# A three-layer transformer forward pass: one attention head, the gates, the turns and the first roundings are given other places in a hand-written order

## What is computed

```python
for layer in range(2):                       # layers one and two
    u = rms_norm(x, attn_norm_w) @ w_in
    o_main = silu(g) * rms_norm(retention(q, k, v))        # layer one, 6 heads
    o_main = rms_norm(diff_attention(q, k, v, lam))        # layer two, 6 heads: softmax(map 0) - lam * softmax(map 1)
    o_mem = memory_attention(qc, mk, mv)                   # both, 4 heads
    x = x + concat([o_main, o_mem]) @ w_out
    x = x + (silu(gate) * up) @ w_down                     # gate, up from rms_norm(x) @ w_gate_up
# layer three
z, xbc, dt, q, k, v, f = split(rms_norm(x) @ w_in_2)
y_ssd = ssd_mixer(silu(causal_depthwise_conv(xbc)), z, dt) # 4 taps, 16 heads
y_fox = fox_mixer(q, k, v, f)                              # 16 heads
x = x + concat([y_ssd, y_fox]) @ w_out_2
x = x + conv_gated_mlp(rms_norm(x))
```

## Time and profile before

| | |
|---|---|
| median of three runs | 1065.42 us |
| the profiled execution | 1065.32 us, its span 1063.5 us |
| TensorE busy | 1042.3 us, 98% of the span |
| VectorE busy | 747.6 us, 70% |
| ScalarE busy | 606.4 us, 57% |
| POOL busy | 155.9 us, 15% |
| data read from HBM | 172.39 MB |

### The profile page before, as it was taken

One profiled execution on the slowest core, in us unless ns is written; L12 is line 12 of the kernel. 1 busy time (PEld: TensorE's weight loads), 2 busy tenths in 40 slices (PEclk: granted clock), 3 DMA queues, 4 the chain that ended last, 5 costly groups with the idle time before them and its releaser, 6 DMA issues.

```text
span 1063.5 us, 23813 instructions
## 1 busy us (share of the span) xinstructions
PE 1042.3 (98%) x8638; PEld 1007.7 (95%) x8638; DVE 747.6 (70%) x1244; ACT 606.4 (57%) x1095; POOL 155.9 (15%) x160
## 2 busy tenths in 40 slices
PE   6999999999999999999999999999999999999998
PEld 6989999999999888999999999999888999999998
DVE  6875886666555877965665549878867479998743
ACT  7654764454544766744445446665766667666532
POOL 2200031111110000311111110000101034454300
PEclk9999999999999999999999999999999999999999
DMA  7533555555655332555555664444233455555563
GB/s 292 179 137 92 168 182 186 185 180 175 190 172 184 133 100 80 181 196 178 186 185 168 190 198 141 165 154 139 95 115 103 147 178 182 191 180 177 175 206 96
DMA packets 51767, 174.43 MB, mean 164 GB/s; under 512 B 5872, under 2 KB 7152, under 8 KB 51568
## 3 DMA queue, kind: packets, MB, share of 16 engines
q1 hardware_dynamic: 51696, 173.46, 49.9%
HBM read 172.39 MB, written 1.05 MB: 163 GB/s over the span
## 4 chain that ended last, share of the span: by engine, by line
PE 52%; DVE 6%; ACT 2%; issue 1%; ACTq 0%; DVEq 0%
PE bank L741 10%; PE bank L742 9%; PE bank L743 9%; PE scores L741 6%; PE scores L742 6%; PE scores L743 6%; DVE ring_lo L1588 2%; DVE xw_lo L1594 1%; ACT tmp L1390 1%; PE scores L947 0%; PE bank L1053 0%; PE bank L970 0%; DVE tmp L1725 0%; DVE x L1686 0%; DVE negmax L1964 0%
## 5 line engine op out<-in xcount | busy, mean ns | idle before, releaser
L1588 DVE TENSOR_TENSOR ring_lo<-ring_raw,ring_hi 128x1024 fp32r<-128x1024 f32 (+2 forms) x340 | 402.7, 1188 | 63.4 <-ACT ring_hi L1120 57.8
L1120 ACT ACTIVATE ring_hi<-ring_raw 128x1024 fp32r<-128x1024 f32 (+2 forms) x340 | 341.3, 1008 | 80.5 <-PE bank L743 39.3
L741 PE MATMUL bank<-xw_hi,ring_hi 128*128 128x256 f32 x1048 | 302.6, 289 | 1.6 <-DVE ring_lo L1588 0.6
L742 PE MATMUL bank<-xw_lo,ring_hi 128*128 128x256 f32 x1048 | 296.3, 283 | 0.0
L743 PE MATMUL bank<-xw_hi,ring_lo 128*128 128x256 f32 x1048 | 296.1, 283 | 0.0
L741 PEld LDWEIGHTS bank<-xw_hi,ring_hi 128*128 128x128 f32 x1048 | 200.5, 191 | 8.1 <-issue 5.1
L742 PEld LDWEIGHTS bank<-xw_lo,ring_hi 128*128 128x128 f32 x1048 | 200.7, 191 | 0.1
L743 PEld LDWEIGHTS bank<-xw_hi,ring_lo 128*128 128x128 f32 x1048 | 200.6, 191 | 0.0
L741 PE MATMUL scores<-xw_hi,ring_hi 128*128 128x256 f32 x528 | 150.1, 284 | 0.1
L742 PE MATMUL scores<-xw_lo,ring_hi 128*128 128x256 f32 x528 | 149.4, 283 | 0.0
L743 PE MATMUL scores<-xw_hi,ring_lo 128*128 128x256 f32 x528 | 149.4, 283 | 0.0
(11 more groups left out here) (238 smaller groups left out, 1792.1 us busy)
## 6 DMA issues: line engine op xcount, KB each, us to landing
ring_raw<-w_up SPq DMA_DIRECT2D x132, 512.0 KB, 3.2
ring_raw<-w_in SPq DMA_DIRECT2D x85, 512.0 KB, 3.3
ring_raw<-w_down SPq DMA_DIRECT2D x48, 512.0 KB, 3.6
ring_raw<-w_down SPq DMA_DIRECT2D x24, 384.0 KB, 3.8
ring_raw<-w_oa SPq DMA_DIRECT2D x24, 256.0 KB, 2.7
ring_raw<-w_ob SPq DMA_DIRECT2D x12, 512.0 KB, 4.1
ring_raw<-w_oa SPq DMA_DIRECT2D x8, 512.0 KB, 3.9
ring_raw<-w_kv SPq DMA_DIRECT2D x7, 512.0 KB, 6.6
```

The source lines that it names most:

```text
L741: mm(bank[b][:, 0:T], w_hi, tile(hi, t), start=kk == 0, stop=False)
L742: mm(bank[b][:, 0:T], w_hi, tile(lo, t), start=False, stop=False)
L1120: A(ring_hi[:, slot * DM:slot * DM + width], ring_raw[:, slot * DM:slot * DM + width], ACT.Copy).then_inc(hi_done, 1)
L1588: V.tensor_tensor(ring_lo[:, a:b], ring_raw[:, a:b], ring_hi[:, a:b].bitcast(f32), SUB).then_inc(lo_done, 1)
```

## The change

- Start: the third tile of `kv` is loaded before the parameters and constants, and ScalarE rounds it after two squares and not after four.
- Layer one: `weights_copy` of the memory heads one slot sooner; `gated` of the second and third pair two slots later (slots 21 and 22 become 23 and 24), their `mix_high` and `mix_low` two and three slots later.
- Layer two: for the sixth head the maxima and the softmax move from before the evacuation or behind the rounding to `MIDDLE`, the copy of the turned weights moves from slot 23 to slot 21 of ScalarE, and the last pair's `mix_low` goes before the rounding of its step.
- `project_group`: in the first `ob` tile both outputs take the first two of their four inputs, then both take the last two.
- Layer three: TensorE turns a tile in the middle of the product tile, not at its end. ScalarE's copies are now called `turn_copy` and stay in their slots.

```diff
-                    at(layer, slot + 2, "weights_copy", "mem", 2 * pair)
+                    at(layer, slot + 1, "weights_copy", "mem", 2 * pair)
...
-        at(0, 20 + half_, "gated", half_)
-        at(0, 21 + half_, "mix_high", 2 * half_)
-        at(0, 21 + half_, "mix_low", 2 * half_)
+        at(0, 22 + half_, "gated", half_)
+        at(0, 23 + half_, "mix_high", 2 * half_)
+        at(0, 24 + half_, "mix_low", 2 * half_)
...
-            plan[1][turned + 1].insert(0, ("weights_copy", "diff", h))
+            at(1, soft, "weights_copy", "diff", h)
...
-        at(2, 4 + t, "turn", 8 + t)
+        at(2, 3 + t, "turn", 8 + t)
+        at(2, 4 + t, "turn_copy", 8 + t)
...
             load_kv(1)
+            load_kv(2)
             sp.dma_start(par[:, streams:NPARAM], params_in[:, streams:NPARAM]).then_inc(par_loaded, 16)
...
-            load_kv(2)
...
-                    for j in range(ph.group):
+                    cuts = (0, ks // 2, ks) if c == 0 else (0, ks)
+                    for k0, k1 in zip(cuts, cuts[1:]):
+                        for j in range(ph.group):
...
-            HALFWAY = (("spread", "turned"), ("spread", "turned"), ("spread", "ssd_out", "small_turn", "fox_turned"))
+            HALFWAY = (("spread", "turned"), ("spread", "turned"), ("spread", "ssd_out", "small_turn", "fox_turned", "turn"))
...
-            for g in range(1, AHEAD):
+            for g, squares_ in ((1, range(0, 2)), (2, range(2, KT))):
...
-            MIDDLE = {"group_out", "norm_mid"}
+            MIDDLE = {"group_out", "norm_mid", "mix_low_mid", "maxima_mid", "softmax_mid"}
```

More of the change, by code:

```diff
@@ L263, in plans @@
         at(1, last, "values", "diff", h)
-        for m in range(2):
-            plan[1][soft].insert(0, ("softmax", "diff", h, 1 - m))
         if h == 5:
+            at(1, soft, "softmax_mid", "diff", h, 0)
+            at(1, soft, "softmax_mid", "diff", h, 1)
             plan[1][turned].insert(0, ("turned", "diff", h))
-            plan[1][turned + 1].insert(0, ("weights_copy", "diff", h))
+            at(1, soft, "weights_copy", "diff", h)
         else:
+            for m in range(2):
+                plan[1][soft].insert(0, ("softmax", "diff", h, 1 - m))
             at(1, turned, "weights", "diff", h)
@@ L539, in program @@
                     k = (layer, *key)
-                    same = {"group_norm": "norm", "weights_copy": "weights", "maxima": "scores"}
+                    same = {"group_norm": "norm", "weights_copy": "weights", "maxima_mid": "scores"}
                     count(same.get(kind, kind), (kind, *k) if kind in ("norm", "group_norm") else k)
@@ L752, in project_group @@
                     pe.wait_ge(lo_done, g + 1)
-                    for j in range(ph.group):
[L754 to L770, removed]
+                    cuts = (0, ks // 2, ks) if c == 0 else (0, ks)
+                    for k0, k1 in zip(cuts, cuts[1:]):
+                        for j in range(ph.group):
+                            m = ph.group * c + j
+                            n = ph.out0 + m
+                            b = bank[ph.bank_of[n]][:, 0:T]
+                            if k0 == 0:
+                                pe.wait_ge(out_ready, ph.freed_out(n))
+                            for k in range(k0, k1):
+                                t = ph.inputs[k]
+                                if m == 0:
+                                    pe.wait_ge(*mixed(layer, t))
+                                a = slot * DM + (j * ks + k) * P
+                                w_hi, w_lo = ring_hi[:, a:a + P], ring_lo[:, a:a + P]
+                                mm(b, w_hi, tile(act_hi, t), start=k == 0, stop=False)
+                                mm(b, w_hi, tile(act_lo, t), start=False, stop=False)
+                                last = mm(b, w_lo, tile(act_hi, t), start=False, stop=k == ks - 1)
+                            if k1 == ks:
+                                last.then_inc(ob_done if j < ph.group - 1 else tile_done, 1)
             def mean_square(q):
@@ L1439, in _ @@
             DO = {"softmax": softmax, "values": values, "fox_probs": fox_probs, "fox_values": fox_values,
-                  "mix_high": mix_high, "weights_copy": weights, "maxima": scores, "small_tok": small_tok, "fox_copy": fox_weights,
-                  "squares": squares, "norm": norm, "group_norm": group_norm, "turn": turn, "decays": decays, "slopes": slopes,
+                  "mix_high": mix_high, "weights_copy": weights, "maxima_mid": scores, "softmax_mid": softmax, "small_tok": small_tok, "fox_copy": fox_weights, "turn_copy": turn,
+                  "squares": squares, "norm": norm, "group_norm": group_norm, "decays": decays, "slopes": slopes,
                   "ret_out": ret_out, "gate_silu": gate_silu, "scores": scores, "weights": weights, "mix": mix,
```

11 lines of the change are left out of this document (6 added, 5 removed).

## The result

The changed kernel takes 1079.24 us (median of four runs, 1076.49 to 1080.18) where the kernel before took 1065.28 us beside it (1064.85 to 1066.02): 14.0 us more, a ratio of 1.0126 with a 95% interval of 1.0106 to 1.0146. Forecast was 1075.2 us, at most 1078.5. The direction and the loop in layer three came as predicted; the time lies 4 us over the forecast and 0.7 us outside its range.

What follows compares the result with a forecast made beforehand. TensorE's products were taken as the bound (busy 1042.3 of 1063.5 us). 1065.3 + 12.7 - 2.4 - 0.5 - 0 - 0 = 1075.1 us profiled, 1075.2 us against the median; 80% range 1072.8 to 1078.5 us.

Steps and rivals of the forecast that it cites:

- The loop: Layer three: each mid-tile turn waits for ScalarE's copy of the one before, 5.19 us per tile; loss 12.7 us.
- The seven waits: Layer three: every turn but the first waits about 2.0 us for the copy, over 14 us in sum.
- a free turn in mid-tile: Rival, layer three: mid-tile turns cost nothing and their 2.0 us of waits go; 1060.5 us, 4%.
- a shorter loop: Rival, layer three: the copy starts 0.8 us sooner, so the loss is about 7.9 us; 1070.4 us, 4%.
- a rival of 12%: Layer three: repeated waits drop TensorE's clock to 1.2 GHz, slowing all seven rounds, 10 us more; 1085 us, 12%.
- Layer two: Sixth head's earlier softmax and copy, and the cut, shorten three TensorE waits: gain 2.4 us, bounds 1.0 to 3.0.
- the first two waits: Layer two: waits for an evacuation (0.92 us) and the turned weights' copy (0.72 us); gains 0.9 and 0.5 us.
- TensorE's third wait: Layer two: 1.38 us wait for the last low part, at 435.32 us; gain 1.0 us.
- Layer one's gates: Output projection: two evacuation waits (0.75 and 0.47 us) mostly go; gain counted 0.5 us, bounds 0 to 1.2.
- The late low part: Layer one's output projection: last low part ready near 129 us, some 0.6 us after TensorE wants it.
- Start and memory copy: Start's wait moves from third to fourth tile, 0 (bounds 0 to 0.9 us); layer one's memory copy, 0 (0 to 0.3).

Runs made afterwards that it cites:

- gates_cut: The kernel before with only layer one's later gates and the cut of the out product's first group: 1064.79 us, ratio 0.9997.

## Why the prediction was right, and where it was not

**The loop: right.** Forecast 5.19 us a round, a second turn at 657.65 and 12.7 us; measured 5.20 us in four of six rounds, 656.92 (TensorE was 0.73 us ahead by then, so this is the forecast place to the hundredth), and 12.95 us where no fall disturbs it. The seven waits came to 12.4 us, not the "over 14" of the text: the turns behind slow products waited 1.31 and 0.84 us, since the loop's length hides part of their slowness. The loop was read from one tile's chain in the earlier trace rows, with no row of the loop itself. Breaking it at the place named, ScalarE's order, takes all of it away. The two other rivals, a free turn in mid-tile and a shorter loop, needed another order on ScalarE; given that order, the free turn came true.

**The step that failed: the clock was left out of the sum.** The text set the fall aside as a rival of 12%, with every round paying. It argued that 1.38 us of idleness in layer two "did not change that", granted that this says nothing of a repeated wait, and then gave the forecast no clock term at all. Measured, the falls cost 2.6 to 3.0 us in the changed kernel and 3.2 us with the turns alone. The right form was between the two: some of the rounds, not none or all. The rival's own sum (10 us) failed as well, in assuming that each of seven rounds pays 1.1 us. In the recorded execution two paid, 0.9 and 0.4 us, and the slow stretch behind the last turn cost 1.5 us, for which the rival had 2. One fall, of 1.5 us more, came where no rival had looked, behind layer two.

**Layer two: mechanism right, size taken at the wrong engine.** Of the first two waits TensorE gained 1.8 us in the trace (1.4 forecast), of the third 1.1 us (1.0 forecast). But the sum stopped at TensorE's third wait. It did not ask who sets the pace behind it: in the trace of the kernel before, VectorE has no idle time from 438.1 to 448.0 us, where the earlier trace rows no longer reaches. Term -2.4, measured -1.3; with POOL's additions left out, -2.65.

**Layer one's gates: -0.5 forecast, 0 measured.** The late low part was seen and its cost put at 0.6 us; the wait is 1.7 us without the cut and 1.1 us with it (the list of waits of `gates_cut`), as much as the waits for evacuations that went. In the changed kernel's own trace it is 0.4 us, so the term can come true in an execution; the medians of the parts show none of it.

**Start and memory copy: right in size.** 0 forecast for both; measured +0.2 and -0.4 us, each within the interval. The wait moved from the third tile to the fourth, and 0.9 us of it is there, as said.

The account closes: 12.95 for the loop, 2.6 to 3.0 for the falls, -1.4 for the rest gives +14.2 to +14.5 us, measured +14.0. Of the 4 us over the forecast, 2.6 to 3.0 are the clock's, 1.1 layer two's, 0.5 the gates', 0.2 each the loop's and the start's, with the memory copy's 0.4 against them: 4.2 to 4.6, as against 14.0 - 9.8 = 4.2 by the medians. The small terms are each within what the medians can tell.

What stays open: why the fall at 448 us comes in more than half of the runs of one kernel and once in eleven of another whose programs are the same up to there; and a second bank for the turns, which was not tried.

## What to carry to other kernels

A step that is moved within one engine's program needs its partner moved too: before a wait for a buffer is put earlier, follow the release of that buffer through the other engine's order, and see whether it hangs on the very work that now stands behind the wait. Where such a loop leaves the matmul engine still again and again, put a part of the falls in the sum, and test it with useless products that fit in the wait; here 8 and 16 of them gave the same time. And a wait removed is worth only what the next engine's pace allows: read the stage behind it for an engine without idle time before crediting the gain.

## What the runs showed of the hardware

Added work made a bound engine's kernel faster: 16 products of 0.12 us in each of seven waits took 3.2 us off (1081.13 to 1077.95 us), 8 did as well (1077.94 us). Waits of about 2.0 us every 5.2 us brought the granted clock to 0.83 or 0.84 in three windows of ten microseconds, waits of about 1.0 us every 5.2 us left it at 1.00.

VectorE's subtraction of two SBUF operands (128 by 1024, fp32) takes 1.22 us alone and 1.76 us beside POOL's additions of 128 by 256, of which two take 2.63 us. The order shows too. In the kernel before, the rounding of 438.57 us, which starts ahead of an addition (439.13), takes 1.21 us; those of 441.39 and 444.69 us, which start 0.3 us behind one, take 1.76 us. The Trainium skill ("SBUF — State Buffer", SBUF: two separate sides) calls the port pair that VectorE and GpSimd share an exclusive lock, which the instruction that starts first holds to its end. The traces fit this in that order and in that the rounding grows by 0.54 us when POOL adds and returns to 1.22 us when the additions are left out; that one blocks the other fully can't be seen here.
